# Gated scan: tree products restricted to their blocks, predicated copies into the attention block, gate sum in PSUM

## What is computed

```python
lg = log_sigmoid((h @ w_g1[d]) @ w_g2[d] + b_g[d]) / 16          # per token, 4 heads x 128
def step(s, inp):                                                # one chunk of a head
    g = cumsum(gc, axis=2)
    decay = exp(where(mask, g[..., :, None, :] - g[..., None, :, :], -inf))
    att = einsum('bhik,bhjk,bhijk->bhij', qc, kc, decay)
    o = einsum('bhij,bhjv->bhiv', att, vc) + einsum('bhik,bhkv->bhiv', qc * exp(g), s)
    g_last = g[:, :, -1:, :]
    s = s * exp(g_last) + einsum('bhjk,bhjv->bhkv', kc * exp(g_last - g), vc)
    return s, o
```

## Time and profile before

| | us |
|---|---|
| median of 3 runs | 3710.23 (3710.05 to 3712.26) |
| the profiled execution | 3710.4 |
| its span | 3708.6 |
| first tree product of the scan, from the span's start | 458.0 |

### The profile page before, as it was taken

One profiled execution on the slowest core, in us unless ns is written; L12 is line 12 of the kernel. 1 busy time (PEld: TensorE's weight loads), 2 busy tenths in 40 slices (PEclk: granted clock), 3 DMA queues, 4 the chain that ended last, 5 costly groups with the idle time before them and its releaser, 6 DMA issues. The chain is left out here.

```text
span 3708.6 us, 48686 instructions
## 1 busy us (share of the span) xinstructions
PE 3321.5 (90%) x17622; PEld 2784.1 (75%) x17622; DVE 2392.6 (65%) x2956; ACT 983.3 (27%) x1352; POOL 1033.1 (28%) x539
## 2 busy tenths in 40 slices
PE   5999988886979999999997768888886899999998
PEld 3789877775768888888885547677775678888886
DVE  7975199999546666666666245656564466666666
ACT  4111233333331111111112424434342131211111
POOL 1332155554122222222221121212111323333331
PEclk8999999998999999999998879999998999999999
DMA  5557200001311111011100100000001111111111
GB/s 205 183 197 244 107 15 1 0 0 42 119 41 41 39 40 34 34 45 38 35 28 12 65 9 5 5 5 5 5 5 68 52 46 51 51 45 51 45 46 57
DMA packets 63019, 196.38 MB, mean 53 GB/s; under 512 B 7553, under 2 KB 19713, under 8 KB 61505
## 3 DMA queue, kind: packets, MB, share of 16 engines
q1 hardware_dynamic: 46064, 164.35, 13.0%
q10 hardware_dynamic: 16848, 30.56, 2.4%
HBM read 176.02 MB, written 18.87 MB: 53 GB/s over the span
## 5 line engine op out<-in xcount | busy, mean ns | idle before, releaser
L1351 DVE SCALAR_TENSOR_TENSOR resid<-ps,mod,resid 128x512 f32<-128x512 f32 (+1 forms) x880 | 602.1, 697 | 471.2 <-PE ps L1247 470.5
L1254 PE MATMUL ps<-hf_hi,up_hi 128*128 128x512 f32 (+1 forms) x1760 | 653.0, 371 | 31.6 <-DVE hf_lo L283 22.6
L1254 PE MATMUL ps<-hf_lo,up_hi 128*128 128x512 f32 (+1 forms) x1760 | 652.1, 370 | 0.0
L1254 PE MATMUL ps<-hf_hi,up_lo 128*128 128x512 f32 (+1 forms) x1760 | 650.4, 370 | 0.0
L1222 POOL TENSOR_SCALAR up_hi<-up_raw 128x1024 fp32r<-128x1024 f32 x88 | 94.5, 1074 | 1160.7 <-PE ps L1254 1099.5
L1254 PEld LDWEIGHTS ps<-hf_hi,up_hi 128*128 128x128 f32 x1760 | 334.7, 190 | 87.8 <-issue 34.4
L1254 PEld LDWEIGHTS ps<-hf_hi,up_lo 128*128 128x128 f32 x1760 | 334.0, 190 | 56.4
L1254 PEld LDWEIGHTS ps<-hf_lo,up_hi 128*128 128x128 f32 x1760 | 335.0, 190 | 51.4
L1247 PE MATMUL ps<-act_hi,dn_hi 128*128 128x512 f32 (+1 forms) x880 | 333.5, 379 | 17.8 <-DVE act_lo L1372 16.1
L1303 ACT ACTIVATE conv<-ps,conv_w 128x1280 f32<-128x1280 f32 (+1 forms) x88 | 115.6, 1314 | 802.4 <-PE ps L1254 802.2
L1247 PE MATMUL ps<-act_lo,dn_hi 128*128 128x512 f32 (+1 forms) x880 | 326.5, 371 | 0.0
(11 more groups left out here) (235 smaller groups left out, 7025.6 us busy)
## 6 DMA issues: line engine op xcount, KB each, us to landing
up_raw<-in_up SPq DMA_DIRECT2D x88, 512.0 KB, 3.3
adaw_ring<-in_adaw SPq DMA_DIRECT2D x80, 512.0 KB, 4.0
dn_raw<-in_dn SPq DMA_DIRECT2D x44, 512.0 KB, 3.3
vr<-vr_out ACTq DMA_DIRECT2D x80, 128.0 KB, 3.1
adaw_first<-in_adaw SPq DMA_DIRECT2D x16, 512.0 KB, 22.0
wvr_raw<-in_wvr SPq DMA_DIRECT2D x8, 1024.0 KB, 7.2
x<-in_xT ACTq DMA_DIRECT2D x8, 640.0 KB, 17.0
r<-vr ACTq DMA_DIRECT2D x10, 512.0 KB, 3.8
```

Source lines behind the costliest of these rows:

```text
L1254: mm = pe.matmul(c.psf[:, at:at + w], a[:, half, k, :], b[:, k, t:t + w], start=(k == 0 and a is up_hi and b is h_hi), stop=(k == KD - 1 a ...
L1351: dve.scalar_tensor_tensor(resid[:, m, t:t + w], c.ps[:, 6 + j % 2, 0:w], c.mod[:, gate + m, cond[t]:cond[t] + 1], resid[:, m, t:t + w], A ...
```

## The change

All of it is in `gla_scan` and the constants it reads.

- Block order: CUM, the seven levels, DIAG, REST. One query product (8 blocks, CUM among them) takes the place of `query` and `query_state`, into one of four buffers; the key product leaves CUM out (9 blocks).
- Levels 0 to 2 are computed only where the mask is 1: one product of 64x64, two of 32x32, four of 16x16 (32x16 in the backward direction), all into one 128x128 block of PSUM. Levels 3 to 6 and the diagonal stay full.
- In place of mask product and reduction, VectorE copies the six blocks of PSUM, each under its mask, into `att`, which is zeroed once. `att` now has a pair of buffers for each direction.
- The tree products give two signals: `coarse_done` after the first four blocks (one PSUM bank) and `tree_done` after the others; TensorE waits for four copies of the unit before ahead of its first product, for six ahead of level 6.
- `fade` and, in fresh steps, the output copy move from VectorE to ScalarE.
- The gate stays in PSUM: ScalarE writes its absolute value to SBUF, exp takes the minus sign as a scale, and VectorE writes the log gate back over the gate in PSUM. One VectorE operation and one ScalarE copy go; ScalarE's absolute value comes.
- The transposed keys move to the free half of the third PSUM bank, behind the last decay bank, with waits on `e_set` and `kt_set`; decay goes bank by bank.
- `w2` is loaded again by a DMA of its own. VectorE's steps are written out; the other engines have three loops where they had one.

```diff
-DIAG, CUM, REST = LEVELS, LEVELS + 1, LEVELS + 2
+CUM, LEVEL, DIAG, REST = 0, 1, 1 + LEVELS, 2 + LEVELS
+NQUERY, NKEY = 1 + LEVELS, 2 + LEVELS
+COARSE = 3
+PICKS = 1 + LEVELS - COARSE + 1
...
-                for n, a in enumerate((lg_hi, lg_lo)):
-                    for t in range(0, NBLK * P, BANK):
-                        m = min(BANK, NBLK * P - t)
+                for t in range(0, NBLK * P, BANK):
+                    m = min(BANK, NBLK * P - t)
+                    if m < BANK and (u >= 2 or not begins(s)):
+                        pe.wait_ge(kt_set, s * U + (u - 1))
+                    for n, a in enumerate((lg_hi, lg_lo)):
...
-                pe.wait_ge(masked_set, s * U + u)
-                for b in range(LEVELS):
-                    pe.matmul(c.psf[:, TREE_PS + b * P:TREE_PS + (b + 1) * P],
-                              kd[u % 2][:, b * P:(b + 1) * P], qd[:, u % 2, b * P:(b + 1) * P],
-                              start=True, stop=True)
+                if not first:
+                    pe.wait_ge(picked, s * (U * PICKS) + (u * PICKS - 2))
+                for b in range(COARSE):
+                    size = P >> b
+                    half = size // 2
+                    for at in range(0, P, size):
+                        keys, queries = (at, at + half) if d == 0 else (at + half, at)
+                        m = half
+                        if keys % 32:
+                            keys, m = at, size
+                        query = (LEVEL + b) * P + queries
+                        pe.matmul(c.psf[keys:keys + m, TREE_PS + queries:TREE_PS + queries + half],
+                                  kd[u % 2][:, b * P + keys:b * P + keys + m],
+                                  qd[:, u % 4, query:query + half], start=True, stop=True)
...
+                for b in range(COARSE, COARSE + 3):
+                    mm = level(b)
+                mm.then_inc(coarse_done, 1)
+                if not first:
+                    pe.wait_ge(picked, s * (U * PICKS) + u * PICKS)
+                for b in range(COARSE + 3, LEVELS + 1):
+                    mm = level(b)
+                mm.then_inc(tree_done, 1)
...
-                dve.tensor_tensor(masked[:, :], c.psf[:, TREE_PS:TREE_PS + LB], mask[:, d, :],
-                                  ALU.mult).then_inc(masked_set, 1)
-                dve.wait_ge(masked_set, s * U + (u + 1))
-                dve.wait_ge(o_done, s * U + (u + 1))
-                dve.tensor_reduce(att[:, u % 2, :], masked[:, :].rearrange("p (b t) -> p t b", t=P),
-                                  AX.X, ALU.add).then_inc(att_set, 1)
+                for n in range(PICKS):
+                    if n == 0:
+                        dve.wait_ge(coarse_done, s * U + (u + 1))
+                    elif n == PICKS - 2:
+                        dve.wait_ge(tree_done, s * U + (u + 3))
+                    dve.wait_ge(picked, (s * U + u) * PICKS + n)
+                    mm = dve.copy_predicated(
+                        att[:, d, u % 2, :], mask[:, d, n * P:(n + 1) * P].bitcast(mybir.dt.int32),
+                        c.psf[:, TREE_PS + n * P:TREE_PS + (n + 1) * P])
+                    mm.then_inc(picked, 1)
...
+            def fading(s, u):
+                last = CUM * P + (P - 1 if u // GH == 0 else 0)
+                act.wait_ge(e_set, s * U + (u + 1))
+                act.wait_ge(s_set, s * U + (u + U - 3))
+                act.activation(fade[:, u % 4:u % 4 + 1], e[:, u % 2, last:last + 1], ACT.Copy
+                               ).then_inc(fade_set, 1)
+            def keep_output(s, u, chunk):
+                d, h = divmod(u, GH)
+                act.wait_ge(o_done, s * U + (u + 3))
+                act.activation(o[:, bass.ds(chunk[d], 1), h * GDV:(h + 1) * GDV],
+                               c.psf[:, O_PS:O_PS + GDV].unsqueeze(1), ACT.Copy).then_inc(o_added, 1)
...
-                dve.scalar_tensor_tensor(lg[:, :], x[:, :], 0.0, lg[:, :], ALU.min, ALU.subtract
+                dve.scalar_tensor_tensor(gate_ps, gate_ps, 0.0, decayed_log[:, :], ALU.min, ALU.subtract
```

More of the change, by code:

```diff
@@ L708, in _, with gla_scan @@
                                   ALU.subtract).then_inc(lg_split, 1)
-def gla_scan(c, qk, v, o, g1, gates, mask_d, vr_d):
+def gla_scan(c, qk, v, o, g1, gates, mask_d, w2_d, vr_d):
     nc, U = c.nc, 2 * GH
[L724 to L735, removed]
-    fade = c.at("fade", 19.75, [P, 4])
[L737 to L743, removed]
@@ new lines, in gla_scan @@
+    tree, g1s, lg_hi, lg_lo = gates.tree, gates.g1s, gates.lg_hi, gates.lg_lo
+    mask = c.at("mask", 151, [P, 2, PICKS * P])
+    state = c.at("state", 157, [P, U, GDV])
+    e = c.at("decay", 165, [P, 2, NBLK * P])
+    w2 = c.at("w2", 175, [64, GH * GDK])
+    decayed_log = c.at("gate_log", 177, [P, GH * GDK])
+    att = c.at("att", 205, [P, 2, 2, P])
+    kt = c.at("k_turned", 179, [P, 2, P])
+    qd = c.at("q_decayed", 189, [P, 4, NQUERY * P])
+    kd = [c.at("k_decayed0", 208, [P, NKEY * P]), c.at("k_decayed1", 218, [P, NKEY * P])]
@@ L749, in ends, with steps, later @@
         return isinstance(s, int) and s == NT - 1
-    def steps(eng, body):
+    def steps(eng, body, unrolled=False):
         L = NT - 1
[L755 to L760, removed]
+        MEET = (L + 3) // 2
+        body(eng, 0, (0, 1), (1, 0), None, True, False)
+        body(eng, 1, (1, 0), (2, L), (0, 1), False, True)
+        body(eng, 2, (2, L), (3, L - 1), (1, 0), True, False)
+        def later(i, back, fresh, prev_fresh):
+            body(eng, i, (i, back), (i + 1, back + (-1)), (i + (-1), back + 1), fresh, prev_fresh)
+        if unrolled:
+            for i in range(3, L):
+                later(i, L + 2 - i, i < MEET, i <= MEET)
+        else:
+            for lo, hi, fresh in ((3, MEET, True), (MEET, MEET + 1, False), (MEET + 1, L, False)):
+                with eng.Fori(lo, hi, 1) as i:
+                    later(i, i * -1 + (L + 2), fresh, lo <= MEET)
+        body(eng, L, (L, 2), None, (L - 1, 3), False, False)
     with c.stage() as block:
@@ new lines, in level @@
+                def level(b):
+                    at = TREE_PS + (1 + b - COARSE) * P
+                    query = (qd[:, u % 4, (LEVEL + b) * P:(LEVEL + b + 1) * P] if b < LEVELS
+                             else qk[:, h, bass.ds(chunk[d] * P, P)])
+                    return pe.matmul(c.psf[:, at:at + P], kd[u % 2][:, b * P:(b + 1) * P], query,
+                                     start=True, stop=True)
+                for b in range(COARSE, COARSE + 3):
+                    mm = level(b)
```

135 lines of the change are left out of this document (59 added, 76 removed).

## The result

The changed kernel takes 3663.1 us (median, 3658.7 to 3667.1) against 3710.1 for the kernel before: a ratio of 0.987, 95% interval 0.986 to 0.988. It is 47 us faster. The forecast was 22 us faster, 3688: the sign is right, and the time lies in its range, but less than half of the gain was foreseen.

A forecast was written before the change was run, and what follows sets the result against it. The prediction took VectorE to bound the gated scan at 5.55 us a unit. Afterwards TensorE and a two-unit chain give 5.33: scan -19.2 us, ends -2.8, so -22 from 3710.2 gives 3688 us, range 3645 to 3725.

The forecast's parts named there:

- VectorE's new work: In the gated scan, VectorE's work falls by 1.65 to 3.9 us a unit, with six predicated copies at 0.32 each.
- busy share of 75% and query mean of 2.5 us: Signs expected in the scan: VectorE busy about 75%, and its query averaging 2.5 us or more, ending behind GpSimd.
- Rival B: Scan copies also read their destination and stop for GpSimd's key product: 5.6 to 5.7 us a unit; chance 0.13.
- TensorE's cycle: TensorE's unit in the scan goes from 4.35 to 4.90 us, and to 6.16 with a gate.
- I take 0.72: Price in us of a unit's fourteen small matmuls on TensorE, taken between bounds of 0.35 and 1.55.
- three changes of tile: TensorE switches to 64 columns, to 32 and back to 128 each unit: 0.17 us each, 0.5 in all.
- The chain over two units: Products, exponential, GpSimd's keys, query, four copies, then products two units later: 10.24 us for two units, 5.12 each.
- port meeting: VectorE's query stands still for GpSimd's key product on a shared SBUF port, ending 1.09 us after it.
- The sum's 419.4: Forecast scan length in us: 71 units at 5.33 plus 8 at 5.12, against 438.6 before.
- cover gone: VectorE's wait at gates for ScalarE's log, if exposed: 0.5 us in 18 units, 9 us; expected hidden behind GpSimd.
- rival A: Small products cheap, no drain on TensorE: about 4.8 to 4.9 us a scan unit, -52 to -60 us; chance 0.24.
- C: Small products cost TensorE as much as full ones: 1.55 + 0.6 us a unit, time 3752 us; chance 0.21.

The follow-up runs named there:

- b1: The kernel before with only the fade copy moved from VectorE to ScalarE: 3707.1 us, ratio 0.999 to the kernel before.
- q4: The changed kernel with the fade and the output copy of fresh steps back on VectorE: 3662.4 us.
- q2: The changed kernel with VectorE's query for the unit after next issued straight behind the copies, and GpSimd waiting for the query before its keys: 3645.1 us.
- n2: The kernel of q2 with each of the fourteen small products issued twice: 3662.5 us.
- n3: The kernel of q2 with levels 3, 4 and 5 each behind the small products of one level, six changes of tile for three: 3684.2 us.
- q1: The changed kernel with VectorE's query for the unit after next issued straight behind the copies, ahead of the state update, without a GpSimd wait: 3683.1 us.
- r2: The changed kernel with only a GpSimd wait for the unit's query added before its keys: 3682.8 us.
- c1: The changed kernel with the same reordering of products as n3: 3690.9 us, scan 29.0 us longer than the changed kernel's.
- n1: The kernel of q2 with three full 128x128 products for levels 0 to 2 in place of the fourteen small ones: 3652.2 us.

## Why the forecast was right and wrong

**What bounds the kernel before.** Right: VectorE. Its row is 99.38, and b1 took 0.05 us a unit off VectorE and 4.0 us off the scan.

**VectorE's new work.** The copies were put at 0.32 and measured 0.348 from start to start, inside 0.25 to 0.45. That VectorE's work would set nothing is confirmed by q4. The forecast's busy share of 75% and query mean of 2.5 us did not come: they are 91 and 2.05, since most queries start when GpSimd is already some way into its keys. Where no query stands still, in q2, the share is 79. Rival B, copies that stop for GpSimd, is excluded. The changed kernel's order of time has six copies mostly under GpSimd's keys, and six mostly ahead of the next keys at 703.95, and they take the same:

```profile
698.05 2.04 DVE L1029 COPY_PREDICATED att<-mask,ps 128x128 f32<-128x128 int32 x6
...
698.76 2.63 POOL L788 TENSOR_TENSOR k_decayed<-decay,qk 128x1152 f32<-128x1152 f32 x1 [1.71 <-ACT decay L951]
...
702.39 2.03 DVE L1029 COPY_PREDICATED att<-mask,ps 128x128 f32<-128x128 int32 x6
```

Over all 80 units six copies take 2.04 at the median, in the 20 units whose copies GpSimd's keys do not touch as in the 29 where they cover about three quarters.

**TensorE's cycle: the step that failed.** "I take 0.72" for the fourteen small matmuls. They cost 0.25 to 0.27 (n2), a third of that, and less than the lower bound of 0.35, which had been scaled from the time of loads by their columns. The bound by columns held for the 64-column ones (0.058 against 0.055) and was too high for the twelve narrower ones. The other term, 0.5 for three changes of tile, was well sized: 0.42 by what is left of 0.67, 0.49 to 0.53 by n3. It rested on the gate's row alone, and the rule of the Trainium skill that stood beside it (TensorEngine Tiling (Array Packing), Key Properties: changing the mode drains TensorE) fits n3, where the same products in another order cost 41 us. From the figure of the Trainium skill (TensorEngine Tiling (Array Packing), Instruction Overhead), about 60 cycles a matmul, one estimates 0.025 us at the 2.4 GHz level; n2 measured 0.018, so the figure is too high here, but nearer than my 0.051. So TensorE's unit is 4.35 - 0.67 + 0.67 = 4.35, not 4.90, and the trace has 4.34 to 4.37. The small products save TensorE nothing and cost it nothing.

**The chain over two units.** Right in its parts. From products to exponential the measured distance is 702.63 - 699.49 = 3.14, and the forecast's 3.80 less 0.55 is 3.25. Exponential to keys 1.32 (1.34 forecast), keys 2.65 (2.63), query 1.08 behind them (1.09), and q1, q2 and r2 show the port meeting from three sides. The query ends 1.08 us behind GpSimd in the median of the 80 units too. The Trainium skill's rule on it (SBUF — State Buffer, Who interferes with whom) agrees with the traces, for the query (1.98 us at the median, 1.23 where it comes first) and for the exempt copies (2.04 and 2.03 above). Putting 0.67 for 1.22 into the forecast's own formulas gives 10.24 - 0.55 = 9.69 for a plain pair and 11.06 - 1.10 = 9.96 for a pair with a gate: 19.65 for four units, 4.91 each, and 4.90 is measured.

**How the one error grew.** A term that was 0.55 us too large made the sum 0.41 us a unit too large, since it counts once in the chain's pair and twice in TensorE's: 1.65 over four units. The sum's 419.4 for the scan is 32 us over the measured 387.3; c1 measured 29 for a price of about the same size.

**Ends and other stages.** The stretch behind the last exponential, to the end of the last state update, fell from 16.1 to 14.0 us, close to the forecast's -2; the first exponential came 0.5 later, where up to 1 us earlier had been put down. So the scan's end came 52.4 earlier. The median of the whole shows 47 of it: some 5 us went in stages that the change leaves alone, as above. The wait for ScalarE's log, 9 us "cover gone", measured 10.4. The forecast had named such a wait as a sign of being wrong, but it costs the scan nothing, as the order of time at one gate shows:

```profile
694.39 2.66 POOL L788 TENSOR_TENSOR k_decayed<-decay,qk 128x1152 f32<-128x1152 f32 x1 [2.82 <-ACT decay L951]
...
695.80 0.70 DVE L1000 SCALAR_TENSOR_TENSOR ps<-ps,gate_log 128x512 f32<-128x512 f32 x1 [0.81 <-ACT gate_log L937]
...
696.41 1.72 DVE L1013 TENSOR_TENSOR q_decayed<-decay,qk 128x1024 f32<-128x1024 f32 x1
```

VectorE gets the log late and starts the query at 696.41, but GpSimd's keys run to 697.05 and the query ends 1.08 behind them (698.13), as it does without a gate.

**Rivals.** The scan came out at the upper edge of rival A's 4.8 to 4.9 us a unit, and the time 5 us above the range that follows from its -52 to -60. But A is only half of what happened. Its products were cheap, cheaper than it said. Its "no drain" is refuted by n3, and its query that wins the port by the changed kernel's own rows (q2 shows what that is worth, 15 us of scan). C, small products at the price of full ones, is refuted by n2 and n1. The chances weighed the unknown price as if 0.11 a matmul were as near as 0.02. Between two bounds from rows of other shapes, 0.35 and 1.55, I took 0.72 for no reason in the rows.

## What to carry to other kernels

A product restricted to its blocks saves TensorE only what the full one costs beyond the changes of tile: here a narrow matmul cost about 0.02 us on average and a change of shape about 0.15, so like shapes are kept together. When an engine is freed, look at whom it now meets. Here VectorE's query came to run against GpSimd's keys, and ordering the two by one more wait, with the query issued early enough, was worth another 18 us; either half alone cost 20. A forecast whose one unknown price decides it should carry that price as the rival, and a kernel in which that engine is the full bound measures it best.

## What the runs showed of the hardware that was not expected

- Narrow fp32 matmuls (16 to 64 key columns, 16 to 64 moving columns) cost 0.018 us each on average at a granted clock of 1.00, where a 128x128 one costs 0.11; the 64-column ones alone stand 0.058 apart. Their records last 0.196 at the median, so the duration tells nothing of the price.
- A change of TensorE's tile shape cost 0.14 to 0.18 us on average, and 0.31 for out of the full shape and in again.
- A predicated copy of 128x128 fp32 from PSUM under an int32 mask in SBUF lasts 0.30 us, stands 0.348 from the next when each waits for the last, and is not slowed by GpSimd.
- A VectorE operation that meets GpSimd counts as busy while it stands still: 91% became 79% with the same work done in less time.
